# Normed input's buffer moved from 64 to 256 bytes under a multiple of 512 bytes

## What is computed

```python
for l in range(DEPTH):                      # DEPTH = 2
    h = rms_norm(x, ffn1_norm_pre[l])
    x = x + 0.5 * rms_norm(swiglu(h, ffn1_w_in[l], ffn1_w_out[l]), ffn1_norm_post[l])
    h = rms_norm(x, mix_norm_pre[l])
    x = x + rms_norm(token_mixer(h, mem, ...), mix_norm_post[l])
    h = rms_norm(x, ffn2_norm_pre[l])
    x = x + 0.5 * rms_norm(swiglu(h, ffn2_w_in[l], ffn2_w_out[l]), ffn2_norm_post[l])
x = ssd_dilated_layer(x, ...)               # input projection, scan, attention, output
x = moba_layer(x, ...)                      # input projection, block attention, output
```

## Time and profile before

| | us |
|---|---|
| median of the runs | 1759.93 |
| the profiled execution | 1758.77 |
| its span, first to last instruction | 1756.9 |
| TensorE matmul busy | 1715.1 (98%) |
| TensorE weight load busy (beside the matmuls) | 1487.3 (85%) |
| VectorE busy | 1260.3 (72%) |
| ScalarE busy | 964.7 (55%) |
| GpSimd busy | 22.7 (1%) |

### The profile page before, as it was taken

One profiled execution on the slowest core, in us unless ns is written; L12 is line 12 of the kernel. 1 busy time (PEld: TensorE's weight loads), 2 busy tenths in 40 slices (PEclk: granted clock), 3 DMA queues, 4 the chain that ended last, 5 costly groups with the idle time before them and its releaser, 6 DMA issues. The chain is left out here.

```text
span 1756.9 us, 28519 instructions
## 1 busy us (share of the span) xinstructions
PE 1715.1 (98%) x10554; PEld 1487.3 (85%) x10554; DVE 1260.3 (72%) x2362; ACT 964.7 (55%) x1630; POOL 22.7 (1%) x21
## 2 busy tenths in 40 slices
PE   7999999999999999999999999999999999899998
PEld 6888899998888888888899988788889878767887
DVE  6666777567876667666876577766677896886775
ACT  5444554665554446444645565544556556563474
POOL 1000000000000000000000000000000000000000
PEclk9999999999999999999999999999999999999999
DMA  8545555634545454554556435454554544204531
GB/s 316 185 180 200 193 192 180 237 135 183 192 185 196 179 216 156 193 201 179 200 197 232 171 125 205 161 209 179 191 201 173 189 155 169 108 1 144 204 120 60
DMA packets 29906, 311.66 MB, mean 177 GB/s; under 512 B 3312, under 2 KB 3696, under 8 KB 4848
## 3 DMA queue, kind: packets, MB, share of 16 engines
q1 hardware_dynamic: 28944, 307.18, 47.1%
q0 software_dynamic: 864, 3.15, 0.5%
HBM read 309.26 MB, written 1.05 MB: 177 GB/s over the span
## 5 line engine op out<-in xcount | busy, mean ns | idle before, releaser
L502 ACT ACTIVATE region_r<-ring 128x1024 fp32r<-128x1024 f32 x505 | 525.0, 1054 | 358.3 <-PE psum L914 333.4
L508 DVE TENSOR_TENSOR ring_r<-ring,region_r 128x1024 fp32r<-128x1024 f32 x496 | 592.3, 1220 | 130.6 <-ACT region_r L502 125.3
L914 PE MATMUL psum<-xs_r,region_r 128*128 128x256 f32 (+2 forms) x3160 | 581.2, 331 | 3.3 <-ACT region_r L502 1.7
L914 PEld LDWEIGHTS psum<-xs_r,region_r 128*128 128x128 f32 (+1 forms) x3160 | 467.4, 188 | 66.0 <-issue 7.8
L914 PE MATMUL psum<-region_r 128*128 128x512 f32 (+3 forms) x1056 | 330.6, 381 | 0.0
L914 PE MATMUL psum<-xs_r,ring_r 128*128 128x256 f32 x2344 | 317.5, 278 | 0.0
L914 PEld LDWEIGHTS psum<-xs_r,ring_r 128*128 128x128 f32 x2344 | 303.8, 188 | 15.8
L914 PE MATMUL psum<-region_r,xs_r 128*128 128x512 f32 (+2 forms) x1056 | 270.3, 349 | 6.2 <-DVE region L2755 3.1
L914 PEld LDWEIGHTS psum<-region_r 128*128 128x128 f32 (+2 forms) x1056 | 193.1, 185 | 36.2 <-DVE region_r L2433 0.6
L914 PEld LDWEIGHTS psum<-region_r,xs_r 128*128 128x128 f32 x1056 | 182.6, 188 | 35.9 <-ACT xs_r L1855 4.5
L914 PE MATMUL psum<-ring_r,region_r 128*128 128x512 f32 (+1 forms) x472 | 169.5, 375 | 0.0
(11 more groups left out here) (250 smaller groups left out, 1558.7 us busy)
## 6 DMA issues: line engine op xcount, KB each, us to landing
ring<-in_weights SPq DMA_DIRECT2D x192, 1536.0 KB, 6.4
gpost<-in_posts POOLq DMA_DIRECT2D x6, 512.0 KB, 4.5
cst<-in_const SPq DMA_DIRECT2D x1, 1213.0 KB, 22.7
PTs<-in_mem SPq DMA_DIRECT2D x1, 1024.0 KB, 5.6
x<-in_x SPq DMA_DIRECT2D x1, 1024.0 KB, 8.0
out<-x SPq DMA_DIRECT2D x2, 512.0 KB, 2.6
pars<-in_par SPq DMA_DIRECT2D x1, 368.0 KB, 6.1
p<-in_par SPq DMA_DIRECT2D x1, 206.0 KB, 22.8
```

Source lines behind the costliest of these rows:

```text
L502: eng.activation(unit.high, unit.like_high(unit.raw), ACT.Copy).then_inc(h_ready, 1)
L508: eng.tensor_tensor(unit.like_high(unit.low), unit.like_high(unit.raw), unit.high.bitcast(F32), ALU.subtract)\
L914: ins = pe.matmul(bank, lhsT, rhs, start=start, stop=stop)
```

## The change

The constant `SHIFT` goes from 16 to 64 words. `before_xs` becomes 64 words long instead of 112, `after_xs` 64 instead of 16, so that `xs` moves down by 192 bytes in each partition and every other buffer keeps its address. `xs` then lies 256 bytes under a multiple of 512 bytes.

```diff
 CHUNK, SLOTS = 3072, 4
-LINE, LEAD, SHIFT = 128, 96, 16
+LINE, LEAD, SHIFT = 128, 96, 64
```

## The result

The changed kernel takes 1772.32 us (median of four runs, 1769.45 to 1775.07) against 1759.35 us (1755.76 to 1761.22) for the one before; the ratio is 1.0077, with a 95% interval of 1.0054 to 1.0100. The profiled execution took 1769.45 us, its span is 1767.6. It is slower, where 1738.5 us had been forecast as the likeliest; the time lies at the top end of the range, at the rival "half the pattern acts as distance 0 does" (1770).

The account below looks back on a forecast made before the run. TensorE was taken as the bound. FFN passes 10.2, down entry 1.7, split tiles 7.1, token blocks 2.1 and branch 0.9 made 22.0 us; without the down entry, 1758.8 - 20.3 = 1738.5 us, range 1734 to 1773.

Parts of the forecast that it names:

- half the pattern acts as distance 0 does: Rival, chance 0.15: 512-column matmuls at 226.7 ns, 256-column ones slowed to 120.0 ns; + 11.2 us, about 1770 us.
- What bounds the kernel: TensorE, busy 1715.1 us of a 1756.9 us span, sets the time; VectorE and ScalarE costed at no change.
- The stalls and their sizes: Surplus of TensorE matmuls over 113.3 and 226.7 ns, tied to operand distance; 22.0 us in all.
- half the pattern: 256 bytes, half of an assumed 512-byte address pattern; forecast clear of stalls, 1734 to 1746 us, chance 0.38.
- split tiles: 124 `split_tile`s of 24 256-column matmuls, about 65 at the slow pace, 2.83 instead of 2.72 us; 7.1 us to win.
- wide highs: 1360 512-column matmuls of `wide_tile` in FFN passes, input in `xs`, 233.8 ns each; 8.8 us to win.
- the floor: Quickest TensorE pace seen in long runs: 113.3 ns for 256 columns, 226.7 ns for 512.
- the 20.3 us: Expected TensorE gain: 22.0 us less 1.7 us on entering the down part, whose operands stay put.
- Wide lows: 1360 256-column matmuls of `wide_tile` in FFN passes, with `ring_r` weights; 1.4 us to win.
- Token blocks: 912 512-column matmuls with `xs` as stationary operand, 229.0 ns each; 2.1 us to win.
- Branch: 384 256-column matmuls of the branch products with `xs` as stationary operand; 0.9 us to win.
- the addresses are not what stalls: Rival, chance 0.19: moving `xs` has no effect on TensorE's matmuls; 1758.8 us, within 3.

Follow-up runs that it names:

- e9: All buffers moved 64 bytes lower than in the kernel before (`LEAD` 80), distances unchanged; 1758.4 us.
- e1: Kernel before with `SHIFT` 0, `xs` at distance 0 from a multiple of 512 bytes, rear filler left out; 1772.9 us.
- e5: Kernel before with `SHIFT` 80, `xs` 320 bytes under a multiple of 512; 1759.5 us.
- e2: Kernel before with `SHIFT` 32, `xs` 128 bytes under a multiple of 512; 1773.2 us.
- e11: Kernel before with `SHIFT` 14; as built, `xs` 32 bytes under a multiple of 512, all buffers behind it 32 above; 1773.1 us.
- e7: Kernel before with `SHIFT` 12; as built, `xs` 32 bytes under a multiple of 512, all buffers behind it 32 above; 1769.8 us.
- e10: Kernel before with `LEAD` 112 and rear filler dropped: `xs` at distance 0, `ring` 64 bytes above a multiple of 512; 1774.7 us.
- e6: Kernel before with `SHIFT` 20; as built, `xs` 64 bytes under a multiple of 512, all buffers behind it 32 above; 1777.0 us.
- e12: Kernel before with `SHIFT` 17; as built, `xs` 64 bytes under a multiple of 512, all buffers behind it 32 above; 1778.1 us.

## Why the prediction was wrong

*What bounds the kernel*: right. TensorE's busy time rose by 11.7 us, the span by 10.7, and nothing hid it. VectorE's low halves went from 1220 to 1221 ns, ScalarE's high parts from 1054 to 1055, as costed.

*The stalls and their sizes*: right as far as seen. The surplus over 113.3 and 226.7 ns changes with the distance between the buffers. Their common place does not matter where all move by 64 bytes (e9, 1758.4 us beside 1758.8), and 256 bytes more do not either (e1 and the change, 1772.9 and 1772.3 us; e5 and before, 1759.5 and 1759). It is not the distance alone, since at 64 bytes one tile has two paces, 113.3 and 117.9 ns. The weight loads of the `ring_r` group are longer at 256 bytes (a mean of 191 ns instead of 188), but not at 128 (188). What on the chip makes the surplus is not shown: no run tells one cause from another, and none keeps the other engines away from these buffers.

*The step that failed* is the one on which the sign hung: that half the pattern is a distance without stalls. It was my estimate, and no row showed it. Nor did a row show the 512 bytes taken for the pattern. The runs repeat after 256 bytes (e1, e5), so that half of 512 is a whole one: the change put the input back to distance 0, whose price stood in the earlier trace rows. I had it in hand as a rival, at 0.15. Its prices, split tiles at 2.88 us beside wide highs at the floor (1.81 us), were seen to the digit. They are the mark of distance 0 and 256, and not of every multiple of 128 bytes, as e2 shows (2.85 and 1.86 us).

*The second thing that failed*: even with the right length no distance clears everything. 128 bytes, half of 256, gives 2.85 us for a split tile and 1.86 for the wide highs. So the idea that half the pattern is clear fails too, and not only the length taken for it. None of the 20.3 us that I counted as to be won came at any of the eight distances tried; 64 and 320 bytes are the best.

*The sizes of the rival that came true*, against what the starts of the same matmuls in the two traces add up to: split tiles + 12.7 us forecast, + 11.3 measured (where nothing interrupts, 62 tiles were at the quick pace and lose 0.16, 62 at the slow one and lose 0.05). Wide lows + 7.7; + 6.3, from 0.915 to 0.95 us a tile. Wide highs - 8.8; - 6.1, from 1.864 to 1.827 us, since the second tile of a pass enters from the lows and needs some matmuls to settle (starts 233, 236, 228, 233 and 230 ns apart, then 227; 1.84 us against 1.81). Token blocks - 2.1; - 1.3. Branch + 1.7; + 0.6. Sum + 11.2 forecast, + 10.8 measured, with + 10.7 in the span. That the sum is so near owes something to errors that cancel. The median rose by 13; the runs at 1774.8 and 1775.1 us had a granted clock of 0.994 and 0.995, those at 1769.5 and 1769.9 of 0.998 and 0.997.

*The count of slow split tiles*, 65, is 62 by the median pace of each tile (the 71 in the expectation of e11 was too many; 71 is the number of quick ones in e7). The large groups with `xs`, called six, are seven.

*The rival "the addresses are not what stalls"* falls: the same instruction stream takes 0.8% longer when one buffer moves (the change itself, 1772.3 us) and as long as before when all move together (e9, 1758.4 us). For the other engines the runs show little: VectorE's low halves took 1220 to 1221 ns at every distance, ScalarE's high parts 1054 to 1058.

*Evidence misread.* The 280-column products with eight distances at 129.0 ns each, half the pattern among them, said that no distance is clear. I gave them the rival "not the addresses"; they were better read as "no distance is free of it": at the floor's pace for 256 columns, 280 would take 123.9 ns (113.3 x 280 / 256).

**What stays open.** Why one distance (64 bytes) has two stable paces, 113.3 and 117.9 ns. In an unbroken row a tile keeps the pace of the one before it; behind a gap the pace can be the other. In the kernel before, wherever a split tile's pace is not that of the last one, two starts ahead of it or in it lie 190 ns or more apart. At 881 us one matmul starts late, some 400 ns behind the one before, in before, e5 and e9 alike; until then all three run at the slow pace, behind it before and e5 go over to the quick one for twelve tiles, and e9, at the same distances, stays slow. What decides there is not shown. That 64 is better than 192 and 128 is measured, but not explained. Whether a placement exists that gives the wide highs their 226.7 ns and the 256-column tiles their 113.3 is open too: the three layouts in which `ring` and `region` lay apart (e10, e7 and e11, e6 and e12) did not give it.

## What to carry to other kernels

Where TensorE is the bound and weights are loaded beside the matmuls, the placement of the two operands is worth about 1% here: put it in the allocation by a constant, keep buffers that take turns within one product at one place of the 256 bytes (down parts and memory values lost 5.0 to 5.3 us where they were not), and measure 0, 64, 128 and 192 bytes of distance, since here 0 and 256 were alike (1772.9 and 1772.3 us) and so were 64 and 320. Only 64 and its like, 320, were quick here; a multiple of 64 is no merit by itself. Read the buffers' addresses in the built program before reasoning from a distance: rounding to 32 bytes moved other buffers in four of these runs. A product that should not have changed and did, like the memory values in e12, gives it away. Read the pace between starts in the timeline, not the mean duration; two paces for one shape are the sign. Before reasoning from half a period, have a row that shows the period, and take the price of the new place from tiles that already stand there: here the memory keys at distance 0 had it to the digit.

## What the runs showed of the hardware

- The pace of fp32r matmuls whose weights are loaded beside the one before: 113.3 ns for 256 columns and 226.7 for 512 at best, 120.0 for 256 columns at distance 0 or 256 bytes, 226.7 there for 512, 113.3 or 117.9 for 256 at 64 or 320 bytes, and 233.5 to 233.8 for 512 columns at 64 under (input moving) and 192 under (input stationary).
- The times repeat after 256 bytes: 1772.3 and 1772.9 us for 256 and 0 bytes, 1759.5 and 1759 for 320 and 64. The other distances tried, 32, 96, 128 and 192, take 1771.2 to 1774.8 us.
- At one placement (64 bytes) equal tiles run at 113.3 or at 117.9 ns, and which of the two can change at a gap in the stream.
- A product whose moving rows lie now at one distance from the stationary tiles, now at another, is slower: the down parts take 2.79 us instead of 2.74 at 32 bytes (e6, e7, e11, e12) and at 64 (e10); in e10 the starts lie 229 to 236 ns apart, 232.7 on average, also where the ring is not read.
